# Gathering tokens for two pairs of experts at once, from slots split by token tile

## The reference, cut to what matters

```
gp = softmax(t @ w_group + b_group);  g_w, g_sel = top_k(gp, 1)
sl = (t @ w_sub + b_sub)[chosen group];  top_p, top_e = top_k(softmax(sl), 2)
expert_id = g_sel * 4 + top_e;  weight = g_w * top_p / sum(top_p)
y = sum over the token's 2 experts of  weight * (silu(t @ w1[e]) * (t @ w3[e])) @ w2[e]
```

## Time and profile before

| | us |
|---|---|
| median of the runs | 1027.51 |
| the profiled execution | 1027.36 |
| its span (first to last instruction) | 1025.4 |
| PE busy | 1000.4 |
| DVE busy | 512.3 |
| ACT busy | 354.5 |

### The profile page before, as it was taken

One profiled execution on the slowest core, in us unless ns is written; L12 is line 12 of the kernel. 1 busy time (PEld: TensorE's weight loads), 2 busy tenths in 40 slices (PEclk: granted clock), 3 DMA queues, 4 the chain that ended last, 5 costly groups with the idle time before them and its releaser, 6 DMA issues.

```text
span 1025.4 us, 15336 instructions
## 1 busy us (share of the span) xinstructions
PE 1000.4 (98%) x5676; PEld 711.1 (69%) x5676; DVE 512.3 (50%) x1398; ACT 354.5 (35%) x861; POOL 86.1 (8%) x140
## 2 busy tenths in 40 slices
PE   6999999999999999999999999999999999999996
PEld 2458554556887777988999877899999744444442
DVE  5559836447265667566865824953534510000004
ACT  5224133435043247245475124842121411111113
POOL 0061000032200004300000000000000010000000
PEclk9999999999999999999999999999999999999999
DMA  9972124762233421364354352058647799999996
GB/s 364 420 299 97 42 82 176 289 275 82 83 123 129 159 82 67 138 231 141 112 204 161 128 199 83 2 189 329 238 190 307 287 396 421 420 421 421 421 419 248
DMA packets 33942, 227.57 MB, mean 222 GB/s; under 512 B 4577, under 2 KB 4849, under 8 KB 8112
## 3 DMA queue, kind: packets, MB, share of 16 engines
q1 hardware_dynamic: 30784, 214.97, 53.3%
q10 hardware_dynamic: 1920, 9.80, 2.6%
q0 software_dynamic: 1168, 1.85, 0.5%
HBM read 222.15 MB, written 8.41 MB: 225 GB/s over the span
## 4 chain that ended last, share of the span: by engine, by line
PE 91%; DVE 6%; ACT 1%; issue 1%; DMA 1%; DVEq 0%; SPq 0%; ACTq 0%
PE lin L669 12%; PE sc L686 11%; PE lin L1398 11%; PE sc L792 6%; PE aux L1398 5%; PE lin L686 4%; PE aux L1246 4%; PE sc L892 4%; PE lin L856 3%; PE sc L1363 3%; PE sc L669 3%; PE aux L922 3%; PE sc L1071 3%; PE lin L908 3%; DVE UN L2281 2%; PE lin L938 2%
## 5 line engine op out<-in xcount | busy, mean ns | idle before, releaser
L669 PE MATMUL lin<-H,ring 128*128 128x256 f32 (+1 forms) x560 | 125.8, 385 | 0.0
L669 PEld LDWEIGHTS lin<-H,ring 128*128 128x128 f32 x560 | 106.0, 190 | 18.0 <-issue 4.2
L792 PE MATMUL sc<-H,ring 128*128 128x512 f32 (+1 forms) x192 | 67.3, 496 | 0.0
L1611 ACT ACTIVATE SP<-lin 128x512 f32<-128x512 f32 (+2 forms) x88 | 42.1, 486 | 71.9 <-PE lin L908 71.9
L2281 DVE SCALAR_TENSOR_TENSOR UN<-UN,cols 128x512 f32<-128x512 f32 (+1 forms) x120 | 66.7, 627 | 0.0
L2193 DVE CUSTOM_DVE_ANT_0 SP<-sc,CW,SK 128x512 f32<-128x512 f32 (+1 forms) x48 | 31.7, 661 | 53.6 <-PE sc L892 53.6
L1622 ACT ACTIVATE SP<-SP,ST 128x513 f32<-128x513 f32 (+4 forms) x88 | 53.9, 612 | 6.7 <-DVE ST L2196 6.4
L792 PEld LDWEIGHTS sc<-H,ring 128*128 128x128 f32 x192 | 34.8, 189 | 30.3 <-issue 25.6
L2848 DVE TENSOR_TENSOR PR<-lin,PR 128x512 f32<-128x512 f32 x8 | 5.5, 692 | 94.5 <-PE lin L1398 94.5
L892 PE MATMUL sc<-PR 64*128 64x256 f32 (+3 forms) x240 | 42.2, 434 | 2.9 <-DVE ST L2193 2.1
L1246 PE MATMUL aux<-Y,ring 128*128 128x256 f32 x192 | 42.0, 379 | 0.2 <-DVE PR L2642 0.2
(11 more groups left out here) (503 smaller groups left out, 1867.6 us busy)
## 6 DMA issues: line engine op xcount, KB each, us to landing
ring<-w_stream SPq DMA_DIRECT2D x119, 1024.0 KB, 6.7
SP<-w_stream SPq DMA_DIRECT2D x14, 1024.0 KB, 20.6
UN<-w_stream SPq DMA_DIRECT2D x10, 1024.0 KB, 19.5
PR<-w_stream SPq DMA_DIRECT2D x8, 1024.0 KB, 17.3
CW<-w_stream SPq DMA_DIRECT2D x8, 1024.0 KB, 17.8
X<-w_stream SPq DMA_DIRECT2D x8, 1024.0 KB, 17.1
Y<-w_stream SPq DMA_DIRECT2D x8, 1024.0 KB, 18.6
PR<-ada_in SPq DMA_DIRECT2D x5, 1024.0 KB, 26.2
```

What stands on the lines that cost most here:

```text
L669: m = mm(dst, w[:, k, :], rhs(k), start=n == 0, stop=n == KT - 1)
L792: m = mm(bank[:, 0:ns * SEQ], filling["w"][:, k, :], H[:, 0:ns, k, :], start=k == 0, stop=k == KT - 1)
L1611: fn(PT[:, g % TURNED, a:b], take()[:, 0:b - a], ACT.Copy).then_inc(lin_taken, 1)
```

## The change

An expert's 64 slots are split by token tile: tile 0 has the first 32 (`HALF`), tile 1 the others, and a token's place is counted within its own tile. The second tile's places therefore no longer need the count of the first tile (one matmul fewer), and the two counts are kept apart. With tiles apart, the selection matrix of one tile needs 32 columns an expert. A gathering matmul of 128 columns now holds four experts, two pairs, and its result goes straight to its tile's columns (128x4x32), with no sum over tiles. For the pairs 0 to 5 (`COUPLED` = 3 times two) tokens are gathered so: the first two pairs ahead of step 0, pairs 2 and 3 in steps 0 and 1, pairs 4 and 5 in steps 2 and 3. Pair 6 is gathered alone in steps 4 and 5, pair 7 alone in step 6, with 64 columns a matmul. The result of two pairs takes all four PSUM banks of `sc`. ACT copies both halves of an odd pair to `TE` behind w3 of the even step. In even steps below 6, nothing stands between w3 and the wait for `e_hidden`; the gather stands behind the transposes, and waits for ACT's copies as well. In step 5 it stands ahead of the transposes alone. ACT's and DVE's first six steps are written out, no longer a loop. The second gate product moves from i = 4 to i = 3.

What follows is the order on PE; names as in the program, `sc`, `lin`, `aux` are PSUM banks. PE in the second block's attention before, from its first scores: rows of L892 are scores, of L669 gate products, of L908 transposes.

Here no gather is left ahead of the transposes. The diff, cut to its core:

```diff
--- before.py
+++ after.py
@@ -59,7 +59,7 @@
 
 PER_STEP = (2, 4)
 
-GATE_STEPS = (1, 4, 7, 10, 13, 16, 40, 42)
+GATE_STEPS = (1, 3, 7, 10, 13, 16, 40, 42)
 EARLY = len(GATE_STEPS)
 LAG = {"l0": 2, "l1": 2, "abm": 2}
 HELD = 6
...
 CAP = 64
+HALF = CAP // TT
 PASSES = SEQ // CAP
+COUPLED = 3
 TABLE = PAIRS * PASSES
 NOWHERE = 4 * P
 EC = PASSES * N_EXP + 2
...
-    c0[:, slice(*C0["first_slot"])] = np.tile(TABLE * (CAP * (e % 2) - 1) + e // 2, TT)
+    c0[:, slice(*C0["first_slot"])] = np.concatenate([TABLE * (CAP * (e % 2) + HALF * t - 1) + e // 2 for t in range(TT)])
...
             bank = aux_bank("places")
             one, before = t0("tri")[:, P:2 * P], t0("tri")[:, 0:P]
             mm(bank[:, 0:16], before, MK1[:, 0, :], start=True, stop=True)
-            mm(bank[:, 16:32], before, MK1[:, 1, :], start=True, stop=False)
-            mm(bank[:, 16:32], one, MK1[:, 0, :], start=False, stop=True).then_inc(aux_ready, 1)
+            mm(bank[:, 16:32], before, MK1[:, 1, :], start=True, stop=True).then_inc(aux_ready, 1)
             bank = aux_bank("counts")
             for tt in range(TT):
-                m = mm(bank[:, 0:16], one, MK1[:, tt, :], start=tt == 0, stop=tt == 1)
+                m = mm(bank[:, 16 * tt:16 * tt + 16], one, MK1[:, tt, :], start=True, stop=True)
             m.then_inc(aux_ready, 1)
...
-            def gather(halves=(0, 1)):
-
-                for half in halves:
-                    for k in range(4):
+            both_pairs = sc.rearrange("p b (a g t n) -> p (b a) g t n", g=4, t=TT, n=HALF)
+            one_pair = sc.rearrange("p b (a g t n) -> p (b a) g t n", g=2, t=TT, n=HALF)
+
+            def gather_both(quarters):
+
+                for q in quarters:
+                    for a in (2 * q, 2 * q + 1):
                         for tt in range(TT):
-                            a = 4 * half + k
-                            m = mm(sc[:, 0, a * P:(a + 1) * P], TK[:, tt, a * P:(a + 1) * P], SEL[:, tt, :],
-                                   start=tt == 0, stop=tt == TT - 1)
+                            m = mm(both_pairs[:, a, :, tt, :], TK[:, tt, a * P:(a + 1) * P], SEL[:, tt, :], start=True, stop=True,
+                                   skip_group_check=True)
                     m.then_inc(e_gathered, 1)
+
+            def gather(half):
+
+                for a in range(4 * half, 4 * half + 4):
+                    for tt in range(TT):
+                        m = mm(one_pair[:, a, :, tt, :], TK[:, tt, a * P:(a + 1) * P], SEL[:, tt, 0:CAP], start=True, stop=True,
+                               skip_group_check=True)
+                m.then_inc(e_gathered, 1)
 
             pe.wait_ge(tk_in, TT)
             pe.wait_ge(e_sel, 1)
-            gather()
+            gather_both(range(4))
...
-                else:
-                    pe.wait_ge(e_sel, i + 2)
-                    gather([0])
+                elif not isinstance(i, int):
+                    pe.wait_ge(e_sel, i - 1)
+                    gather(0)
+                elif i == 2 * COUPLED - 1:
+                    gather(1)
+                elif i % 2:
+                    gather_both([2])
                 pe.wait_ge(e_hidden, i + 1)
...
-                else:
-                    gather([1])
+                elif not isinstance(i, int):
+                    gather(1)
+                elif i % 2 == 0:
+                    pe.wait_ge(e_te_in, 2 * i + 4)
+                    pe.wait_ge(e_sel, i // 2 + 2)
+                    if i == 2 * COUPLED - 2:
+                        gather(0)
+                    else:
+                        gather_both([0, 1])
+                elif i < 2 * COUPLED - 1:
+                    gather_both([3])
                 pe.wait_ge(e_hid_in, i + 1)
...
-            def gathered(n, halves=(0, 1)):
-                for half in halves:
-                    act.wait_ge(e_gathered, 2 * n + half + 1)
-                    fn(TE[:, 4 * half:4 * half + 4, :].rearrange("p k n -> p (k n)"), sc[:, 0, half * 512:(half + 1) * 512],
-                       ACT.Copy).then_inc(e_te_in, 1)
-
-            gathered(0)
+            both_pairs = sc.rearrange("p b (a q n) -> p (b a) q n", q=2, n=P)
+            one_pair = sc.rearrange("p b (a n) -> p (b a) n", n=P)
+
+            def gathered(n, half, landed):
+
+                act.wait_ge(e_gathered, landed)
+                a = slice(4 * half, 4 * half + 4)
+                src = both_pairs[:, a, n % 2, :] if isinstance(n, int) and n < 2 * COUPLED else one_pair[:, a, :]
+                fn(TE[:, a, :], src, ACT.Copy).then_inc(e_te_in, 1)
+
+            for half in range(2):
+                gathered(0, half, 2 * half + 2)
 
             def experts(i, last=False):
                 act.wait_ge(e_first, i + 1)
                 fn(SG, lin[0][:, :], ACT.Silu).then_inc(e_silu, 1)
                 if not last:
-                    gathered(i + 1, [0])
+                    act.wait_ge(e_third, i + 1)
+                    if not isinstance(i, int):
+                        gathered(i + 1, 0, 2 * i + 3)
+                    elif i % 2 == 0:
+                        for half in range(2):
+                            gathered(i + 1, half, 2 * i + 4)
+                    else:
+                        gathered(i + 1, 0, 2 * i + (3 if i == 2 * COUPLED - 1 else 4))
                 act.wait_ge(e_turned, i + 1)
...
-                    gathered(i + 1, [1])
+                    if not isinstance(i, int):
+                        gathered(i + 1, 1, 2 * i + 4)
+                    elif i % 2:
+                        gathered(i + 1, 1, 2 * i + (4 if i == 2 * COUPLED - 1 else 6))
...
-            with act.Fori(0, last_pair) as i:
+            for i in range(2 * COUPLED):
+                experts(i)
+            with act.Fori(2 * COUPLED, last_pair) as i:
                 experts(i)
...
-                for x in range(2):
-                    ins = v.tensor_scalar(SEL[:, tt, x * CAP:(x + 1) * CAP], t0("iota"), 1.0, RF["place"][:, tt, x:x + 1], ALU.add, ALU.is_equal)
+                for x in range(4):
+                    ins = v.tensor_scalar(SEL[:, tt, x * HALF:(x + 1) * HALF], t0("iota")[:, 0:HALF], 1.0, RF["place"][:, tt, x:x + 1],
+                                          ALU.add, ALU.is_equal)
...
+            def chosen(n, pairs):
+
+                for tt in range(TT):
+                    for x in range(2 * pairs):
+                        ins = v.tensor_scalar(SEL[:, tt, x * HALF:(x + 1) * HALF], t0("iota")[:, 0:HALF], PX[:, tt, bass.ds(2 * n + x, 1)],
+                                              None, ALU.is_equal)
+                ins.then_inc(e_sel, 1)
+
+            def shares(n):
 
                 for tt in range(TT):
                     for x in range(2):
-                        w = CX[:, tt, bass.ds(2 * n + x, 1)] if weight else None
-                        ins = v.tensor_scalar(dst[:, tt, x * CAP:(x + 1) * CAP], t0("iota"), PX[:, tt, bass.ds(2 * n + x, 1)], w,
-                                              ALU.is_equal, *([ALU.mult] if weight else []))
-                ins.then_inc(done, 1)
+                        a = x * CAP + tt * HALF
+                        ins = v.tensor_scalar(SW[:, tt, a:a + HALF], t0("iota")[:, 0:HALF], PX[:, tt, bass.ds(2 * n + x, 1)],
+                                              CX[:, tt, bass.ds(2 * n + x, 1)], ALU.is_equal, ALU.mult)
+                ins.then_inc(e_sw, 1)
...
-                    slots(SW, i, True, e_sw)
-                else:
+                    after(step(v.memset(SW[:, :, :], 0.0)))
+                    shares(i)
+                elif not isinstance(i, int):
                     dve.wait_ge(e_gathered, 2 * i + 2)
-                    slots(SEL, i + 1, False, e_sel)
+                    chosen(i + 1, 1)
+                elif i % 2 == 0:
+                    dve.wait_ge(e_gathered, 2 * i + 4)
+                    chosen(i + 2, 1 if i == 2 * COUPLED - 2 else 2)
```

More of the change, by code:

```diff
@@ L179, in constants @@
     c0[:, slice(*C0["iota"])] = np.arange(CAP)
-    c0[:, slice(*C0["caps"])] = CAP * np.arange(1, PASSES)
+    c0[:, slice(*C0["caps"])] = HALF * np.arange(1, PASSES)
     c0[:, slice(*C0["fold"])] = i[:, None] % 32 == np.arange(2)
@@ L2761, in _ @@
             for tt in range(TT):
-                for x in range(2):
-                    ins = v.tensor_scalar(SEL[:, tt, x * CAP:(x + 1) * CAP], t0("iota"), 1.0, RF["place"][:, tt, x:x + 1], ALU.add, ALU.is_equal)
+                for x in range(4):
+                    ins = v.tensor_scalar(SEL[:, tt, x * HALF:(x + 1) * HALF], t0("iota")[:, 0:HALF], 1.0, RF["place"][:, tt, x:x + 1],
+                                          ALU.add, ALU.is_equal)
             ins.then_inc(e_sel, 1)
-            v.tensor_reduce(CN[:, 0:1], take("counts")[:, 0:16], AX.X, ALU.max).then_inc(aux_taken, 1)
+            v.tensor_reduce(CN[:, 0:1], take("counts")[:, 0:32], AX.X, ALU.max).then_inc(aux_taken, 1)
             dve.wait_ge(aux_taken, at["aux"])
@@ L2785, in places @@
```

(23 more changed lines are left out.)

## The result

The change made the kernel slower. It took 1030.22 us (median of 12 runs, 1029.14 to 1030.86), the kernel before 1027.4 us in runs beside it (1026.88 to 1028.22): a ratio of 1.0025, interval 1.0018 to 1.0032, so a quarter of a percent, small but clear of the noise. Forecast were 1026.5 us and a range to 1027.8. The profiled execution took 1029.45 us, its span is 1027.6 us, 2.2 us longer than before.

A forecast was written before the change was run, and what follows sets the result against it. PE's chain, the full weights' stream and DVE's row blocks behind it end within 3 us of each other. Gate product 0.5 + end 0.4 + experts' start 0.1 = 1.0 us saved: 1026.5 us, range 1024.0 to 1027.8.

The forecast's parts named there:

- The experts' saving: PE's gathers and transposes in the expert steps: 8.1 us saved in sum, bounds 6 and 10, before waits for weights.
- The gate product: Second block's attention: the moved product covers PE's 1.05 us wait for DVE; 0.5 us gained, bounds 0 and 1.05.
- The tail: Kernel's end: DVE stays bound by the row blocks and gains only its waits for PE, 0.4 us, bounds 0 and 2.9.
- The step that failed: Weights' stream in the experts: no faster, full from 811 on, same bytes, so row blocks still land from 1010.6 on.
- the 2.9 us forecast for w3 of the last pair: Last expert pair: PE takes the last w3 unit at 999.4, ending w3 at 1001.1 instead of 1004.01.
- The signs that the prediction named for being wrong: First sum well before 1009.5, PE without waits for DMA, or PE's clock falling before the last matmul.
- (a): Attention and kernel's end: nothing arrives, DVE's order eats 0.5 us and ACT's squares 0.4; 1027.5 us, chance 0.06.
- (b): Kernel's end: row blocks land early enough and only the weights bind, 2.9 + 0.5 + 0.1; 1024.0 us, chance 0.09.
- (d): Attention: the product ahead of scores 2 holds up DVE, +1.2 us; slower, 1029 us, chance 0.04.
- (c): Experts: the stream is not at its limit and the whole saving comes through, 8.1 + 0.6; 1018.8 us, chance 0.04.
- (e): Last expert pair: gaps make PE's clock fall to 1.2 GHz, 14.4 us of matmuls take twice that; 1038 us, chance 0.04.
- (f): Experts' gathers: the strided output doubles a gather's price, the first ending 3.6 us later; 1029 us, chance 0.03.

The follow-up runs named there:

- tile 1 from the top: The changed kernel with tile 1's slots counted from the top of their 32 (rank r takes slot 31 - r): 1026.98 us, ratio 0.9995 to the kernel before.
- the constant table: The changed kernel with constant row numbers, 64 live rows per stored pair at the even partitions: 1026.36 us, ratio 0.9989.
- p < 64: The kernel before with constant row numbers, the 64 live rows of each stored pair at partitions 0 to 63: 1030.34 us, ratio 1.0027.

## Why the prediction was wrong

**The experts' saving** was right in kind and a sixth too high: 5.96 us over the first five steps (124.93 before, 118.97 after), 7.05 forecast. Step 0 saves 25.0 - 24.21 = 0.8 us for 1.05, step 1 25.0 - 23.53 = 1.5 for 1.95, step 3 25.0 - 23.17 = 1.8: in step 1 VectorE's product starts 0.4 us late (the issue at 852.88), which I had not counted. None of this made a difference at the end. That 64 columns cost the full price of 128 came true: the half gather of step 4 takes 1.73 us for 16 instructions (925.09), and 16 of 128 columns take 1.79.

**The gate product** was right. The chain of waits after, beside the earlier trace rows:

```profile
613.42 0.70 PE sc L894 x4
614.13 0.65 PE lin L910 x4
614.78 0.37 PE aux L924 x4
615.14 1.93 PE sc L671 x8
```

The third product starts at 615.14 for 615.66, and the experts at 814.87 for 815.41. Of the 0.1 us for their start nothing shows: the first gather begins 0.7 us sooner (811.12 for 811.84) and takes 0.18 longer, which is 0.54 in all. VectorE's first selection lies within its bounds, in the upper half:

```profile
809.65 1.26 DVE L2804 TENSOR_SCALAR PR<-c,RO 128x32 f32<-128x32 f32 x8
```

**The tail** was right in kind. VectorE's chain is bound by the row blocks, and the waits for TensorE before the last two additions are gone, as the timeline above shows.

**The step that failed** is this one: "The stream does not get faster: it is full from 811 on, its bytes are the same", and from it "stand behind the same bytes, and still land from 1010.6 on". Full it is, and its bytes are the same, but that does not fix when they land. The term was set to 0 and measures about +3.2 us (1030.22 less 1026.98, the two layouts of the changed kernel; 4.0 us in the kernel before, 1031.22 less 1027.25). The same step was behind the 2.9 us forecast for w3 of the last pair, and of these none came: its last weights were forecast to land at 999.4, and TensorE waits for them until 1002.23. With the term taken out, the rest of the sum is not contradicted, nor is it shown: -1.0 forecast, -0.3 measured with an interval of -1.4 to +0.5. I had followed what the change does to TensorE's and VectorE's instructions and to the number of bytes, and had not asked which partitions the slots go to. I could have: the layout stood in the diff, and the Trainium skill's section named above gives a map, though for another kind of transfer. By it the fullest engine goes from 40 rows to 56. At the 0.156 us worked out above that is 2.5 us (an estimate), and the sum would have been +1.5, slower. The signs that the prediction named for being wrong did not help either: they look for a first sum that begins too early, not for one that begins late.

**The rivals.** (a), (b) and (d) did not come: the row blocks did not land early, and VectorE was not held up in the attention. (c) is half true in a way that I did not see: the stream was at its limit, but the saving does come through, 4.6 us of it, once its row writes are gone. (e) is excluded: in both windows above, 875 to 990 and 990 to 1010, with TensorE's gaps between short bursts in them, the granted clock stayed at 1.00, the upper level. (f) is excluded: the first gather with the strided output takes 3.75 us for 3.57. No rival named the row write's placement, and my range ended at 1027.8 since all slower cases hung on the engines' instructions. A range to 1031 would have needed one rule: a full stream can also get slower.

**A version that beats both?** The changed kernel with tile 1 from the top is 3.2 us faster than the change, but against the kernel before it can't be told from no change. With all engines even (28 rows, by the constant table) it would be 1 us under the kernel before, which bounds what a still better permutation can give. The gate product alone, at 1026.61, can't be told from either.

## What to carry to other kernels

Where a stream of transfers is the bound, its share and GB/s over all engines don't say when a transfer lands: ask for every other transfer in the stretch which of the 16 engines it loads, and count the fullest. A look at the last microseconds of the stream is quicker still: a busy share that falls to a half or a quarter there, while transfers are still awaited, means that few engines hold the rest. An indirect or masked transfer whose live partitions form a pattern (the first half of every 32, the lower 64) puts its bytes on few engines; a change of layout on the compute side is then also a change of the stream. And where two bounds are of one height, leaving out one of them in a run of its own (here: no rows) tells what each is worth before anything is built on it.

## What the runs showed that I had not expected

- The partitions on which the live rows of an indirect write lie change the time by 3 to 4 us for 1.85 MB in a kernel that moves 227.56 MB; what counts is how many rows fall on one engine, and a map with bits 3, 4 and 6 of the partition, without bits 0 and 5, fits all runs. The rows that are out of bounds cost little: with next to no rows stored the changed kernel takes 3.65 us less than with 28 on each engine, and the bytes of 28 rows alone would take 4.4 at 0.156 each.
- One wrong map of partitions on engines (M2) fitted two runs, another (M1) six. M2 fell to two layouts made for it, M1 only to the last, p < 64. The map that stands fits all seven, but so does one with bit 1 in place of bit 2.
- A stretch with a DMA share of 1.01 and 421 GB/s, the same in both kernels, hid a delay of 3 us. It shows as a lower rate only at the end (990 to 1010: 0.98 and 405 GB/s; before, in the same view, 1.01 and 416), and plainly in 1010 to 1012, 0.52 for 0.94.
